# Differential attention values projected into token order, with the tokens as the stationary operand

## What is computed

```python
h = x * (1 + scale) + shift
proj = h @ p['w_in'][l]
hy_in, da_q, da_k, da_v, mla_dq, mla_dkv, mla_kr, paths, merge = jnp.split(proj, IN_SPLITS, axis=-1)
...
v = da_v.reshape(b, n, DA_HEADS, DA_V_DIM)      # 4 heads x 128 = 512 columns
...
def diff_attention(q, k, v, lam):
    s = jnp.einsum('bqjhd,bkjhd->bjhqk', qb, k) * scale
    pr = jax.nn.softmax(s, axis=-1)
    pr = pr[:, 0] - lam * pr[:, 1]
    return jnp.einsum('bhqk,bkhe->bqhe', pr.astype(v.dtype), v)
```

## Time and profile before

| | before |
|---|---|
| device time, three runs | 2184.79, 2186.32, 2188.69 us; median 2186.32 us |
| profiled execution, span first to last instruction | 2188.1 us (mean granted TensorE clock 0.972); the page gives no other time for it |
| TensorE matmul busy | 2072.3 us (95%), 11844 records |
| VectorE, ScalarE, GpSimd busy | 1030.0, 634.1, 517.6 us |
| HBM traffic | 67 GB/s over the span |

### The profile page before, as it was taken

How to read it: one execution, slowest core, us unless ns; L and a number is a source line. 1 busy time by engine, 2 the same in 40 slices (tenths; PEclk the granted TensorE clock), 3 DMA queues, 4 the chain that set the end, 5 groups by cost and what they waited for, 6 DMA issues and landing times.

```text
span 2188.1 us, 28690 instructions
## 1 busy us (share of the span) xinstructions
PE 2072.3 (95%) x11844; PEld 1743.4 (80%) x11844; DVE 1030.0 (47%) x1486; ACT 634.1 (29%) x1075; POOL 517.6 (24%) x248
## 2 busy tenths in 40 slices
PE   6899999999999999999989999999999999999995
PEld 4578689887896778699976786898788777778995
DVE  3548587344343343321256676844443444442325
ACT  2221222334323333322133222123332233342221
POOL 0221124221231111154222111331222311013541
PEclk9999999999999999999989999999999999999997
DMA  8001012111211111232531010221112111112331
GB/s 316 30 30 39 29 49 87 53 44 38 93 59 49 56 49 68 73 106 83 168 126 39 29 39 30 68 66 51 39 49 102 44 32 39 49 44 74 129 116 48
DMA packets 45760, 149.44 MB, mean 68 GB/s; under 512 B 6590, under 2 KB 8126, under 8 KB 44480
## 3 DMA queue, kind: packets, MB, share of 16 engines
q1 hardware_dynamic: 45632, 147.62, 20.2%
HBM read 141.02 MB, written 6.59 MB: 67 GB/s over the span
## 4 chain that ended last, share of the span: by engine, by line
PE 79%; DVE 11%; ACT 3%; issue 2%; POOL 2%; DMA 1%; SPq 1%; DVEq 0%; ACTq 0%; POOLq 0%
PE PS L686 16%; PE PS L691 16%; PE PS L687 16%; PE PS L739 6%; PE PS L722 5%; PE PS L755 5%; PE PS L857 3%; PE PS L710 3%; PE PS L969 2%; PE PS L768 2%; PE PS L824 1%; DVE work L1650 1%; ACT work L1022 1%; PE PS L959 1%; DVE work L1648 1%
## 5 line engine op out<-in xcount | busy, mean ns | idle before, releaser
L1601 POOL TENSOR_TENSOR Wl<-W,Wh 128x1024 fp32r<-128x1024 f32 x196 | 438.4, 2239 | 1464.7 <-ACT Wh L1022 1438.6
L686 PE MATMUL PS<-Hh,Wh 128*128 128x320 f32 x2112 | 636.7, 316 | 8.8 <-ACT Wh L1022 3.8
L687 PE MATMUL PS<-Hl,Wh 128*128 128x320 f32 x2112 | 624.7, 310 | 0.0
L686 PEld LDWEIGHTS PS<-Hh,Wh 128*128 128x128 f32 x2112 | 399.3, 189 | 35.0 <-issue 21.7
L687 PEld LDWEIGHTS PS<-Hl,Wh 128*128 128x128 f32 x2112 | 399.6, 189 | 2.5 <-issue 1.2
L691 PE MATMUL PS<-Hh,Wl 128*128 128x320 f32 x2112 | 331.4, 309 | 0.9 <-POOL Wl L1601 0.9
L691 PEld LDWEIGHTS PS<-Hh,Wl 128*128 128x128 f32 x2112 | 315.1, 188 | 1.4 <-POOL Wl L1601 1.4
L1022 ACT ACTIVATE work<-PS 128x640 f32<-128x640 f32 (+9 forms) x266 | 171.5, 654 | 403.4 <-PE PS L722 99.6
L1255 DVE TENSOR_REDUCE st<-PS 128x1 f32<-128x640 f32 (+1 forms) x160 | 114.8, 718 | 197.1 <-PE PS L739 148.5
L1022 ACT ACTIVATE Wh<-W 128x1024 fp32r<-128x1024 f32 x196 | 185.8, 950 | 52.6 <-PE PS L691 27.0
L739 PE MATMUL PS<-work 64*128 64x320 f32 (+1 forms) x512 | 157.7, 440 | 4.2 <-DVE work L1553 2.3
(11 more groups left out here) (174 smaller groups left out, 2569.3 us busy)
## 6 DMA issues: line engine op xcount, KB each, us to landing
W<-in_w_in SPq DMA_DIRECT2D x132, 512.0 KB, 3.5
W<-in_w_mod SPq DMA_DIRECT2D x32, 512.0 KB, 3.6
W<-in_w_branch SPq DMA_DIRECT2D x48, 256.0 KB, 2.6
pmod_w<-in_w_mod SPq DMA_DIRECT2D x8, 1024.0 KB, 17.2
W<-in_w_out SPq DMA_DIRECT2D x16, 512.0 KB, 3.6
work<-in_x_sample SPq DMA_DIRECT2D x2, 2048.0 KB
x_mid<-work SPq DMA_DIRECT2D x1, 2560.0 KB, 9.1
work<-x_mid SPq DMA_DIRECT2D x1, 2560.0 KB
```

The source lines that it names most:

```text
L686: pe.matmul(out, Wh[:, b, kk, :], xh[:, kk, t], start=kk == 0, stop=False)
L687: pe.matmul(out, Wh[:, b, kk, :], xl[:, kk, t], start=False, stop=False)
L1601: return pool.tensor_tensor(out, in_, high.bitcast(f32), ALU.subtract)
```

## The change

`v` is computed the other way round: 128 tokens are stationary and 512 weight columns (all four heads) stream, so the result is already in token order. Five steps `v` 0 to 4 (one for each 128 tokens) of 24 matmuls each take the place of four `v` and four `vt`. All four weight tiles must be in place for the first of them, so they get buffers of their own, `Wvh` and `Wvl` [128, 8, 512], filled by new steps `vw` 0 to 3, which own the tiles and are work for ScalarE and GpSimd alone. These stand between the `qk` steps, and leave the rings of `Wh` and `Wl` out. The result goes straight from PSUM to `V` on ScalarE. The cached keys' landing place `ckc` moves to another address.

```diff
@@ layer_steps
     s += [("qk", c) for c in range(8)]
-    for c in range(4):
-        s += [("v", c)] + ([("kc", 0), ("sk", 0)] if c == 0 else [])
-        if c:
-            s += [("vt", c - 1)]
-    s += [("vt", 3)]
+    s = s[:-6] + [("vw", 0), s[-6], ("vw", 1), s[-5], ("vw", 2), s[-4], ("vw", 3)] + s[-3:]
+    s += [("kc", 0), ("v", 0), ("sk", 0)] + [("v", t) for t in range(1, NT)]
...
+VW = SPLIT_AT["vw", 0]
+RING = [n for n, (kind, _) in enumerate(SPLIT) if kind != "vw"]
...
+        Wvh = sb("Wvh", [128, KD, 512], f32r, over=work_at + 4 * 8704)
+        Wvl = sb("Wvl", [128, KD, 512], f32r, over=work_at + 4 * 12800)
...
+        def ring(n):
+
+            return RING.index(n) % 2
+
+        def ring_free(l, n):
+
+            at = RING.index(n) - 2
+            return filled(l, *SPLIT[RING[at]]) if at >= 0 else filled(l - 1, *SPLIT[RING[at]])
...
@@ TensorE
                     elif kind == "v":
-                        project(l, kind, i, Hh, Hl, KD)
-                    elif kind == "vt":
-                        pe.wait_ge(*freed(l, kind, i))
-                        ps = slot(l, kind, i)
-                        pe.wait_ge(*after("raw_ready", l, 9 + i))
-                        for t in range(NT):
-                            last = transpose(ps[:, 128 * t:128 * t + 128], raw[:, i % 2, 128 * t:128 * t + 128])
+                        pe.wait_ge(*freed(l, kind, i))
+                        out = slot(l, kind, i)[:, 0:512]
+                        pe.wait_ge(*after("w_hi", l, VW + 4))
+                        toks = slice(128 * i, 128 * i + 128)
+                        for kk in range(KD):
+                            pe.matmul(out, Hh[:, kk, toks], Wvh[:, kk, :], start=kk == 0, stop=False)
+                            pe.matmul(out, Hl[:, kk, toks], Wvh[:, kk, :], start=False, stop=False)
+                        pe.wait_ge(*after("w_lo", l, VW + 4))
+                        for kk in range(KD):
+                            last = pe.matmul(out, Hh[:, kk, toks], Wvl[:, kk, :], start=False, stop=kk == KD - 1)
                         last.then_inc(full_of(l, kind, i), 1)
@@ ScalarE, high_part
                 act.wait_ge(w_here[g % NW], 16 * (g // NW + 1))
+                if SPLIT[n][0] == "vw":
+                    c = 128 * SPLIT[n][1]
+                    if c == 0:
+                        act.wait_ge(*filled(l, "inv", 7))
+                        act.wait_ge(*after("y_ready", l, 2))
+                    copy(Wvh[:, :, c:c + 128], W[:, g % NW]).then_inc(sems["w_hi"], 1)
+                    return
                 if l or n >= 2:
-                    act.wait_ge(*tile_done(l, n - 2))
+                    act.wait_ge(*ring_free(l, n))
...
@@ ScalarE, step v
+                    elif kind == "v":
+                        act.wait_ge(*filled(l, kind, i))
+                        copy(V[:, 1 + i, :], slot(l, kind, i)[:, 0:512]).then_inc(sems["v_ready"], 1)
@@ VectorE
-                    elif kind == "vt":
-                        dve.wait_ge(*filled(l, kind, i))
-                        ps = slot(l, kind, i)
-                        dve.tensor_copy(V[:, 1:6, 128 * i:128 * i + 128],
-                                            ps[:, 0:640].rearrange("p (a b) -> p a b", a=NT)).then_inc(sems["v_ready"], 1)
@@ GpSimd, low_part
                 pool.wait_ge(*after("w_hi", l, n + 1))
+                if SPLIT[n][0] == "vw":
+                    c = slice(128 * SPLIT[n][1], 128 * SPLIT[n][1] + 128)
+                    minus(Wvl[:, :, c], W[:, g % NW], Wvh[:, :, c]).then_inc(sems["w_lo"], 1)
+                    return
```

More of the change, by code:

```diff
@@ L159, in owned @@
 def owned(kind, i):
-    first = {"conv": T_HY, "path": T_PATH, "mgate": T_MERGE, "qk": T_Q, "v": T_V, "dqkv": T_DQ, "kr": T_KR}
+    first = {"conv": T_HY, "path": T_PATH, "mgate": T_MERGE, "qk": T_Q, "vw": T_V, "dqkv": T_DQ, "kr": T_KR}
     if kind in ("nmod", "gmod"):
@@ L441, in build @@
         OT = area(work, 14080, 4, NTOK)
-        ckc = area(work, 16640, 512)
+        ckc = area(work, 19200, 512)
         stk = area(work, 17152, 512)
@@ L638, in _ @@
                         sp.wait_ge(*after("sk_ready", l, 1))
-                        sp.wait_ge(*after("v_ready", l, 4))
+                        sp.wait_ge(*after("v_ready", l, NT))
                         sp.dma_start(o_k[0, l].rearrange("t a h d -> t (a h d)"), stk).then_inc(store_k, 16)
@@ L911, in _ @@
                         if i == 0:
-                            pe.wait_ge(*after("v_ready", l, 4))
+                            pe.wait_ge(*after("v_ready", l, NT))
                         pe.wait_ge(*after("da_pt", l, NT * (i + 1)))
@@ L1037, in high_part @@
                 act.wait_ge(w_here[g % NW], 16 * (g // NW + 1))
+                if SPLIT[n][0] == "vw":
[5 more added lines that the diff above has]
+                    return
                 if l or n >= 2:
-                    act.wait_ge(*tile_done(l, n - 2))
+                    act.wait_ge(*ring_free(l, n))
                 k = CT if SPLIT[n][0] == "mbranch" else KD
-                copy(Wh[:, n % 2, 0:k, :], W[:, g % NW, 0:k, :]).then_inc(sems["w_hi"], 1)
+                copy(Wh[:, ring(n), 0:k, :], W[:, g % NW, 0:k, :]).then_inc(sems["w_hi"], 1)
             for l in range(DEPTH):
@@ L1122, in _ @@
                            .then_inc(sems["th_ready"], 1)
-                    elif kind in ("qk", "v"):
-                        n = i + 8 * (kind == "v")
+                    elif kind == "qk":
                         act.wait_ge(*filled(l, kind, i))
                         ps = slot(l, kind, i)
-                        if n >= 10:
-                            act.wait_ge(*after("v_ready", l, n - 9))
-                        elif n >= 2:
-                            act.wait_ge(*after("qk_ready", l, n - 1))
-                        copy(halves(raw[:, n % 2, 0:NTOK]), two(ps), DA_SCALE if n < 4 else 1.0).then_inc(sems["raw_ready"], 1)
+                        if i >= 2:
+                            act.wait_ge(*after("qk_ready", l, i - 1))
+                        copy(halves(raw[:, i % 2, 0:NTOK]), two(ps), DA_SCALE if i < 4 else 1.0).then_inc(sems["raw_ready"], 1)
+                    elif kind == "v":
+                        act.wait_ge(*filled(l, kind, i))
+                        copy(V[:, 1 + i, :], slot(l, kind, i)[:, 0:512]).then_inc(sems["v_ready"], 1)
                     elif kind == "kc":
@@ L1467, in _ @@
                         dve.wait_ge(*own("qk_ready"))
-                    elif kind == "vt":
-                        dve.wait_ge(*filled(l, kind, i))
-                        ps = slot(l, kind, i)
-                        dve.tensor_copy(V[:, 1:6, 128 * i:128 * i + 128],
-                                            ps[:, 0:640].rearrange("p (a b) -> p a b", a=NT)).then_inc(sems["v_ready"], 1)
-                        dve.wait_ge(*own("v_ready"))
                     elif kind == "da_score":
```

15 lines of the change are left out of this document (6 added, 9 removed).

## The result

| | before | changed |
|---|---|---|
| median of all runs | 2187.5 us (4 runs, 2184.8 to 2190.6) | 2199.4 us (4 runs, 2197.6 to 2202.9) |
| ratio | 1 | 1.0057, 95% interval 1.0042 to 1.0072 |
| span of the profiled execution | 2188.1 us | 2195.6 us |

The account below looks back on a forecast made before the run. TensorE, busy 95% of the span, was taken as the bound. Per layer 8.0 - 6.3 - 0.4 = +1.3, so +2.6 us; clock falls +6.8; total +9.4 on the median 2186.3 gives 2195.7 us, range 2187.5 to 2201.5.

Parts of the forecast that it names:

- The gaps, 8.0 us a layer: Before `qk` 2 to 5 TensorE waits for a late `Wh`: four gaps of 2.00 us, loss 8.0 us a layer.
- The new matmul, 0.215: In the `v` steps: a 512-column matmul takes 0.215 us, half of a float32 record's 0.430; 120 take 25.8 us.
- a column costs the same at 512: Rival on the `v` matmuls: 0.235 us for 0.215, +4.8 us; 2200.5, or 2193.7 with the clock held; chance 0.08.
- 0.294 is 2 x 0.1467: Step pricing the `v` matmul: float32 records, 0.294 us at 320 columns, take twice the split type's 0.1467.
- Its warning that the matmuls would gain next to nothing: By the skill page's formula the `v` matmuls would gain 0.2 us a layer, not 2.4.
- Transposes and waiting, 3.9 a layer with the gap of `v` closed: Stage end: `v` 0-1 gap of 2.00 us, 20 transposes (2.19) and 0.6 waiting go; eight transposes (0.87) stay.
- at the first scores: VectorE does `lamc` early, so TensorE's idle time before the next projection goes: gain 0.4 us a layer.
- The clock, +6.8 us: Behind the new gaps before `qk` 2 to 5: clock falls in half of eight, 1.7 us each, +6.8 us.
- at 1.74 one of two fell: Step for the clock: after 1.74 us idle, 24 records took 12.26 us in layer 0, 10.57 in layer 1.
- the clock holds: Rival for the new gaps: one fall at most, 2188.9 us, up to 2190.6; chance 0.25.
- Costed at nothing: Around the `qk` and `v` steps: GpSimd's low parts, loads, VectorE's rotary work and `v` copies cost no time.
- the new gaps hold the clock because the old one did: If transposes don't count as busy, the old `v` 0-1 gap was as empty and held: 2188.9 us.

Follow-up runs that it names:

- Experiments 1: Changed kernel with the table rewritten so that the `Wh` of every `qk` is again made one projection early: 2176.7 us, ratio 0.9940 to the kernel before.
- experiments 2: Kernel before with only the `Wh` of `qk` 2 to 5 made late, behind the copy of the `qk` before: 2205.5 us, ratio 1.0072.
- Experiment 5: Changed kernel with bfloat16 operands in the `v` matmuls, still 512 columns: 2190.3 us in one run.
- experiment 7: Kernel before with the `Wh` of `v` 1 prepared one projection early: 2182.2 us against 2188.8, ratio 0.9975.
- experiments 3: Kernel before without the 20 transposes of `v` a layer, values left untransposed: 2188.9 us against 2189.6, ratio 0.9991.
- experiments 3 and 4: The second of these: kernel before without the transposes of `v`, and VectorE's `lamc` operations moved to step `kc`: 2181.1 us against 2188.8, ratio 0.9962.
- experiments 2, 5 and 6: The last of these: the changed kernel unedited, timed and traced again: 2198.4 us against 2188.8 for the kernel before, ratio 1.0043.
- experiment 11: Kernel before with the `Wh` of `qk` 2 to 5 made late and one eight-column ScalarE copy ahead of each: 2219.6 us in one run.
- Experiment 12: Kernel before with two eight-column ScalarE copies ahead of the `Wh` of `v` 1 alone: 2186.1 us in one run.
- experiments 8: Kernel before with the `Wh` of `qk` 2 to 5 made late and each copied twice: 2224.1 us in one run.
- experiments 8 and 9: The second of these: kernel before with the `Wh` of `qk` 2 to 5 late and copied twice, that of `v` 1 copied twice too: 2226.9 us, one run.

## Why the prediction was right, and where it was not

The sign and the size came out: +9.4 us forecast for the medians, 9.5 and 11.9 measured, and 2199.4 lies inside the range. Two terms of the sum were wrong, in opposite directions (4.6 us too little and 6.8 too much in the two layers). That they nearly cancel is luck.

- **The gaps, 8.0 us a layer: right.** The price, 2.00 each, was read off `v` 0 and `v` 1, and so were their number and place. Experiments 1 and 2 show it by taking the gaps away and by adding them alone.
- **The new matmul, 0.215: wrong.** It takes 0.234, so "a column costs the same at 512" is what happened, the rival I gave 0.08, and with the held clock its 2193.7 is the case that came true. The matmuls gained nothing (28.1 us for 28.16). The failed step is "0.294 is 2 x 0.1467": it took the mean of a short run for the pace. The first two of those 8 records lie 0.37 apart and the rest 0.269, and the piece of the chain takes in the change to other work as well. The pace shows in the middle of the first scores, and in another group with 320 columns, both in the timeline of TensorE:

```profile
415.60 2.58 PE L739 MATMUL PS<-work 64*128 64x320 f32 x9
...
675.61 3.39 PE L969 MATMUL PS<-work 128*96 128x320 f32 x12
```

  9 records take 2.58 and 12 take 3.39, the last ending 0.43 after its start: (2.58 - 0.43) / 8 = (3.39 - 0.43) / 11 = 0.269, or 0.42 ns a column and stream, the same as at 512. With these rows the extra cost of some 8% shows as one of the split type (0.458 ns a column at 320), to be carried to 512 unchanged. Experiment 5 shows it on the chip: same columns, short type, 0.216. The term was 0.019 x 120 = 2.3 us a layer too good, 4.6 in all.
- **"TensorE: Matmul & The Clock Gate", "Back-to-back issue gap",** the page of the Trainium skill weighed in the prediction, gives 216 ns at 512 columns, as the gap of a single matmul by itself: that is bfloat16's 0.216 in experiment 5, and not the split type's 0.234. The about 131 ns that the section gives for a stream of loads and matmuls at 512 columns are not borne out by the stream of experiment 5, 0.216. Its warning that the matmuls would gain next to nothing came true for another reason than the one it gives.
- **Transposes and waiting, 3.9 a layer with the gap of `v` closed: right in sum.** Measured are 3.7 (4.25 less the 0.50 at the first scores, where the term was 0.4, and less 0.06 of the matmuls). The gap closed is 1.13 (experiment 7). The 20 transposes and the waits around them are the rest. That they would be won only with VectorE free was the term "at the first scores"; experiments 3 and 4 show that without it half of them is lost to an idle time and the other half to the clock that falls behind it. The term read the 1.55 us of `lamc` as that operation's own; it is time in which GpSimd's subtraction runs.
- **The clock, +6.8 us: wrong.** It fell in none of the eight gaps, nor in 24 others of the same 1.74 us (experiments 2, 5 and 6). The failed step is "at 1.74 one of two fell", carried over from a place where five transposes and a short wait stand ahead of the idle time. The rate read there from two cases was fair (11 of 28 in all traces), the place was not like the new gaps (0 of 32). What is shown is how near it was: at 1.98 it fell in six of eight (experiment 11), and behind scores at 1.60 in two of two (experiment 3). As a rival "the clock holds" had 0.25, with 2188.9; with the true price of a column it becomes 2188.9 + 4.6 = 2193.5.
- **Costed at nothing:** the low parts, the loads, VectorE's rotary work and the copies of `v` held nobody up. The rotary work had little to spare: it ends at 396.34, and the transposes of `sk` start at 396.49.

By these terms the median should be 2186.3 + 7.5 = 2193.8, or 7.5 above that of before. Measured are 2199.4 and 2198.4, 11.9 and 9.5 above. The profiled execution of the change was its fastest of four, and that of experiment 6 the third fastest of eleven (2191.5), so their spans understate the medians; before's span of 2188.1 lies above the median of its runs (2187.5). No trace shows the 2 to 4 us that are left: outside the stage the two traces agree, and experiment 6's is 6 us shorter. Its interval (5.9 to 12.7 us) takes in 7.5; that of the first measurement (9.2 to 15.8) does not. That the forecast of +9.4 comes so near the measured medians is in part luck too: without its term of the clock it had +2.6.

Experiment 12 was made for the rule of "Part 4: PE-mode transpose", on the same page, that transposes don't count as busy for the clock. It doesn't bear the rule out (2.21 us without a projection's matmul, clock held twice), and neither do the 32 places with five transposes between projections, where it held behind up to 2.45 us. The 11 falls in 28 would fit the rule, but have another difference beside them. What the prediction drew from the rule, that the new gaps hold the clock because the old one did, came true; by these rows it did so for another reason.

## What to carry to other kernels

When a step is put between others, follow the table that prepares operands ahead: preparation tied to "the next owner's place" silently becomes preparation behind a wait. Here this cost 16 us, and a table corrected in a few lines turns 0.6% slower into 0.6% faster. Price a new shape from rows of the same type, and if none has the size, compare two types at two sizes before carrying a ratio over, by the distance inside a run of records and not by the mean of a short one. A saving just ahead of a meeting point of two engines is worth only what the other engine can follow, and the idle time that it leaves can cost the clock as well.

## What the runs showed of the hardware that was not expected

- Split-type matmuls cost 0.458 ns a column at 320 and 512 columns alike (0.1467 and 0.234 us); bfloat16 0.216 us at 512 and float32 twice 0.215.
- TensorE's clock behind gaps in a row of projections: idle 1.74 us, 0 falls in 32 (changed kernel, experiments 2, 5, 6); 1.98 us, 6 in 8 (experiment 11); 2.83 us, 11 in 16 (experiments 8 and 9). A fall cost 1.5 us as a rule, 1.3 at least and 2.7 at most. In experiments 8, 9 and 11 the fourth gap of each layer held every time; why is open.
- Behind 16 score matmuls and an idle time of 1.60 us it fell in 2 of 2 (experiment 3), at 1.5 us each.
- With five transposes between two projections it held behind idle times of 1.58 to 1.90 us in 32 of 32. An idle time of 1.74 us with five transposes and a wait of 0.46 just ahead and float32 work behind let it fall in 11 of 28 cases, at 1.7 us each (12.26 for 10.57).
- An operation of VectorE on a single column with two sources, 0.16 us by itself, took 1.55 and 1.98 us where it met GpSimd's subtraction, and ended 0.02 us behind it (kernel before, experiment 3). No run takes the subtraction alone away.
